# Layer 0's output projection in two parts, the first beside the threshold search, and layer 1's weight highs on another engine

## The reference

```python
h = rmsnorm(x, ev_norm)                       # then one input projection
ya = bg * causal_dwconv(cg * hv, conv_w)      # mixer A: features 0..511
yb = indexed_sparse_attention(...)            # mixer B: features 512..1023; top 256 keys by an indexer
x = x + concatenate([ya, yb]) @ w_out         # w_out: 1024 x 1024
x = x + conv_ffn(rmsnorm(x, ffn_norm), ...)   # D_FF = 2816
```

## Time and profile before

| what | us |
|---|---|
| median of 3 runs (2313.43 to 2315.07) | 2313.96 |
| the profiled execution's own time | 2312.72 |
| its span in the profile | 2310.9 |
| PE busy (share of the span) | 2127.4 (92%) |
| DVE busy | 1286.1 (56%) |
| POOL busy | 1098.9 (48%) |
| ACT busy | 940.6 (41%) |

### The profile page before, as it was taken

One profiled execution on the slowest core, in us unless ns is written; L12 is line 12 of the kernel. 1 busy time (PEld: TensorE's weight loads), 2 busy tenths in 40 slices (PEclk: granted clock), 3 DMA queues, 4 the chain that ended last, 5 costly groups with the idle time before them and its releaser, 6 DMA issues. The chain is left out here.

```text
span 2310.9 us, 29711 instructions
## 1 busy us (share of the span) xinstructions
PE 2127.4 (92%) x11534; PEld 1037.7 (45%) x11534; DVE 1286.1 (56%) x1955; ACT 940.6 (41%) x1385; POOL 1098.9 (48%) x729
## 2 busy tenths in 40 slices
PE   6989737899899999999989999679989999999998
PEld 3544325644344444444434444464434444444444
DVE  8788888735774156416634032884676416631652
ACT  5458956703562055215313212651355215521520
POOL 5113214124884667457585032013588456745642
PEclk8999969999999999999999999769999999999999
DMA  4002100011122112211232011002012111121112
GB/s 165 19 10 55 28 1 1 20 44 47 37 55 66 46 53 57 71 55 38 71 98 55 0 37 37 1 20 64 28 38 72 55 54 55 55 64 46 55 34 93
DMA packets 185986, 109.82 MB, mean 48 GB/s; under 512 B 3871, under 2 KB 180422, under 8 KB 185878
## 3 DMA queue, kind: packets, MB, share of 16 engines
q1 hardware_dynamic: 185414, 107.00, 15.9%
q0 software_dynamic: 464, 1.39, 0.2%
HBM read 104.18 MB, written 4.19 MB: 47 GB/s over the span
## 5 line engine op out<-in xcount | busy, mean ns | idle before, releaser
L626 POOL TENSOR_SCALAR w_scaled<-stage 128x1024 f32<-128x1024 f32 (+1 forms) x100 | 107.4, 1074 | 814.2 <-PE ps L890 504.5
L969 PE MATMUL ps<-h_hi,arena 128*128 128x512 f16 x1280 | 391.3, 381 | 11.6 <-DVE arena L2326 6.5
L890 PE MATMUL ps<-arena,w_hi 128*128 128x512 f16 x1504 | 388.0, 381 | 10.4 <-POOL w_lo L629 7.8
L969 PE MATMUL ps<-arena 128*128 128x512 f16 x1440 | 317.4, 379 | 0.1
L2282 DVE SCALAR_TENSOR_TENSOR xT<-ps,xT 128x1024 f32 (+1 forms) x64 | 78.3, 1224 | 409.3 <-PE ps L890 362.4
L969 PE MATMUL ps<-h_lo,arena 128*128 128x512 f16 x640 | 243.9, 381 | 0.0
L2335 DVE SCALAR_TENSOR_TENSOR work<-ps,fvec,work 128x1023 f32<-128x1023 f32 (+1 forms) x176 | 221.4, 1278 | 26.5 <-ACT work L1619 23.4
L890 PEld LDWEIGHTS ps<-arena,w_hi 128*128 128x128 f16 x1504 | 147.0, 98 | 191.0 <-POOL w_lo L629 11.2
L890 PE MATMUL ps<-arena,w_lo 128*128 128x512 f16 x752 | 224.6, 380 | 0.0
L969 PEld LDWEIGHTS ps<-arena 128*128 128x128 f16 x1440 | 140.8, 98 | 170.4 <-POOL arena L701 1.0
L969 PEld LDWEIGHTS ps<-h_hi,arena 128*128 128x128 f16 x1280 | 125.8, 98 | 166.5 <-issue 14.7
(11 more groups left out here) (363 smaller groups left out, 3819.9 us busy)
## 6 DMA issues: line engine op xcount, KB each, us to landing
stage<-in_ffn_w_up_dram SPq DMA_DIRECT2D x76, 512.0 KB, 4.2
stage<-in_ffn_w_down_dram SPq DMA_DIRECT2D x32, 512.0 KB, 4.2
stage<-in_od_w_in_dram SPq DMA_DIRECT2D x20, 512.0 KB, 3.7
stage<-in_ev_w_in_dram SPq DMA_DIRECT2D x12, 512.0 KB, 3.8
arena<-in_ffn_w_up_dram SPq DMA_DIRECT2D x12, 512.0 KB, 4.8
stage<-in_ffn_w_down_dram SPq DMA_DIRECT2D x16, 384.0 KB, 3.4
arena<-in_x_dram SPq DMA_DIRECT2D x8, 512.0 KB, 7.7
stage<-in_ev_w_out_dram SPq DMA_DIRECT2D x8, 512.0 KB, 3.9
```

The lines of the kernel that those rows point to most:

```text
L626: nc.gpsimd.tensor_scalar(scaled, src, W_SCALE, 1.0, ALU.mult, ALU.mult).then_inc(w_parts, 1)
L890: last = mm(out2[:, hf * HALF:(hf + 1) * HALF], w, a[:, k0 + k, hf * HALF:(hf + 1) * HALF], start=(first and k == 0 and pss == 0), stop=(l ...
L969: last = mm(ps[:, bank, :], left, right[:, k, :], start=(fresh and k == 0 and pss == 0), stop=(k == 3 and pss == 2), skip_group_check=True)
```

## The change

Layer 0's output projection runs in two parts. The first, `ev_out_a`, takes feature tiles 0 to 2 (of mixer A) of all eight units: it has eight unit numbers, eight ring uses and eight loads (192 KB) of its own, its splits stand on GpSimd between the mixer units' and the picks, and its matmuls on TensorE between the last mixer unit and the scores. VectorE adds each finished tile to `xT` in `add_early`: five in bits 26 to 30, one behind the search, one inside `resolve`, one behind it. `resolve` now stands ahead of `attend`. The scores wait for all eight adds. The second part takes feature tiles 3 to 7 where the whole was. Apart from that, the high parts of six of layer 1's eight token-major weight tiles (1 to 6) go from GpSimd to ScalarE, woven into its squares of the last down units.

```diff
-RESOLVE_AT = 1
+EARLY_KS = 3
+EARLY_BIT = 26
...
+        early_added, EARLY0 = rope_act, 7
...
-        order = [("ev_tm", 8, 0), ("ev_sc", 12, 12), ("ev_out", 8, 8), ...
+        order = [("ev_tm", 8, 0), ("ev_sc", 12, 12), ("ev_out_a", 8, 8), ("ev_out", 8, 8), ...
...
+        TM_HIGH_BY_ACT = (1, 2, 3, 4, 5, 6)
...
-            stream("ev_out", 2, 4, lambda i, u: (col_unit(t["ev_w_out"][0], i * 2 * P + u * P), 8))
+            stream("ev_out_a", 2, 4, lambda i, u: (col_unit(t["ev_w_out"][0], i * 2 * P + u * P)[:, 0:EARLY_KS], EARLY_KS))
+            stream("ev_out", 2, 4, lambda i, u: (col_unit(t["ev_w_out"][0], i * 2 * P + u * P)[:, EARLY_KS:], KT - EARLY_KS))
...
-                nc.gpsimd.tensor_scalar(hi, src, W_SCALE, 1.0, ALU.mult, ALU.mult).then_inc(w_parts, 1)
+                if not hi_by_act:
+                    nc.gpsimd.tensor_scalar(hi, src, W_SCALE, 1.0, ALU.mult, ALU.mult).then_inc(w_parts, 1)
                 pool.wait_ge(w_parts, n * 2 + 2)
...
-                        split(n, s, stage[:, s, :], w_scaled[:], otw_hi[:, i, :], otw_lo[:, i, :])
+                        split(n, s, stage[:, s, :], w_scaled[:], otw_hi[:, i, :], otw_lo[:, i, :], hi_by_act=i in TM_HIGH_BY_ACT)
...
             split_section("ev_sc", 6, 2, peeled=6)
+            split_section("ev_out_a", 2, 4, words=lambda u: EARLY_KS * P)
...
-            split_section("ev_out", 2, 4)
+            split_section("ev_out", 2, 4, words=lambda u: (KT - EARLY_KS) * P)
...
+            pe.wait_ge(a_mix, EARLY_KS)
+            for m in range(KT):
+                if m == 0:
+                    pe.wait_ge(a_f, 5)
+                elif m == 1:
+                    pe.wait_ge(a_cg, 5)
+                else:
+                    pe.wait_ge(early_added, EARLY0 + m - 1)
+                pe.wait_ge(w_split, unit0["ev_out_a"] + m + 1)
+                three_pass(m % 2, EARLY_KS, mix_hi, mix_lo, 0, pair(m % 2), True, True).then_inc(unit_done, 1)
+
             pe.wait_ge(a_f, 6)
+            pe.wait_ge(early_added, EARLY0 + KT)
...
-            out_projection("ev_out", 0, mix_hi, mix_lo, [(0, 8)], {})
+            out_projection("ev_out", 0, mix_hi, mix_lo, [(EARLY_KS, KT - EARLY_KS)], {})
...
-                residual_squares(24, 2)
+                for m in range(KT):
+                    if m + 1 in TM_HIGH_BY_ACT:
+                        n = woven("tm", m + 1)
+                        act.wait_ge(w_landed[n % 2], n * 8 + (16 - 8 * (n % 2)))
+                        act.wait_ge(w_split, n)
+                        A(otw_hi[:, m + 1, :], stage[:, n % 2, :], ACT.Copy, scale=W_SCALE).then_inc(w_parts, 1)
+                    act.wait_ge(x_added, m + 27)
+                    act.wait_ge(sq_added, m + 14)
+                    A(work[:, m % 2, :], xT[:, m, :], ACT.Square).then_inc(sq_ready, 1)
...
-            def resolve():
+            def resolve(between):
...
                 ts_(V.copy_predicated(back, srch_i[:, S_TAKE, allc], tr_))
+                between()
...
+            def add_early(m):
+
+                dve.wait_ge(unit_done, ring0["ev_out_a"] + m + 1)
+                V.scalar_tensor_tensor(out=xT[:, m, :], in0=pair(m % 2), scalar=W_UNSCALE, in1=xT[:, m, :],
+                                       op0=ALU.mult, op1=ALU.add).then_inc(early_added, 1)
+
             def mixer_part(bit):
+                if bit >= EARLY_BIT:
+                    add_early(bit - EARLY_BIT)
...
-                    if n == RESOLVE_AT:
-                        resolve()
...
             for bit in range(SEARCH_BITS):
                 search_bit(bit, lambda: mixer_part(bit))
+            add_early(KT - 3)
+            resolve(lambda: add_early(KT - 2))
+            add_early(KT - 1)
             attend()
+            dve.wait_ge(early_added, EARLY0 + KT)
```

More of the change, by code:

```diff
@@ L315, in build @@
         nu = nr = 0
-        order = [("ev_tm", 8, 0), ("ev_sc", 12, 12), ("ev_out", 8, 8), ("up0", 2, 2), ("plain0", 0, 2),
+        order = [("ev_tm", 8, 0), ("ev_sc", 12, 12), ("ev_out_a", 8, 8), ("ev_out", 8, 8), ("up0", 2, 2), ("plain0", 0, 2),
                  ("down0a", 8, 8), ("down0b", 8, 8), ("down0c", 0, 8), ("od_r_a", 0, 2),
@@ L616, in _, with split @@
             assert steps[0] == ROPE_STEPS, steps
-            def split(n, slot, src, scaled, hi, lo, ring=None):
+            def split(n, slot, src, scaled, hi, lo, ring=None, hi_by_act=False):
                 pool.wait_ge(w_landed[slot], n * 8 + (16 - 8 * slot))
```

## The result

The changed kernel takes 2290.48 us (median of 4 runs, 2289.36 to 2291.15) beside 2313.69 us of the kernel before on the same chip: 0.9899 of its time, 95% interval 0.9882 to 0.9916, or 23.2 us less. A second measurement on another chip gave 2291.40 beside 2313.88 us (0.9903, 0.9887 to 0.992). The forecast was 2288.0, with 2282 to 2298 as its range. Its form was right, part by part. What it lacked is a term for stretches whose code does not change.

What follows compares the result with a forecast made beforehand. TensorE was taken to bound the output projection, VectorE and ScalarE the search, GpSimd's period the woven stretch; -31.1 + 9.6 - 4.5 = -26.0 us from the 2313.96 us median gave 2288.0 us, range 2282 to 2298.

Steps and rivals of the forecast that it cites:

- Part 1: Output projection behind the attention: each of 8 units loses 18 of 48 matmuls, -31.1 us, bounds -31.1 and -28.
- supply rival: Output projection: load and split in series hold five-tile units at 10.35 us, no gain there, 2319.1 us; chance 0.04.
- rival that ends slower: The same weight-supply case in the output projection: the only one slower than before, deciding from a 9.7 us period; chance 0.04.
- Part 2: Early units in search and attention start: eight adds on VectorE and later head masks cost +9.6 us, bounds +8 and +13.
- head chain: Attention start: scores, mask to exp, exp to turn, turn put head 2's mask 1.9 us behind the last add.
- cold-units rival: Early units: pauses keep TensorE at 1.2 GHz throughout, VectorE waits for units, +8.6 us, 2296.6 us; chance 0.08.
- collision that the prediction had allowed for: Search with mixer: GpSimd's early splits collide with a VectorE tap pass or low part, 0 to 0.9 us, 0.3 taken.
- Part 3: Woven stretch: ScalarE makes six high parts, GpSimd's period falls from 8.97 to 8.0 us, -4.5 us, bounds -6 and 0.
- upper bound of -6: Woven stretch: GpSimd's low part stops colliding with VectorE's sum and TensorE sets 7.8 us per unit, -6 us.
- rival that the highs bring nothing: Woven stretch: square and high in one ScalarE queue delay the adds as much as GpSimd gains, 2292.5 us; chance 0.12.
- The sum: Whole kernel: -31.1 + 9.6 - 4.5 = -26.0 us, giving 2288.0 us.
- condition named in advance: Attention from head 2's mask to its end: a change in length of over 2 us would make the forecast wrong.

Runs made afterwards that it cites:

- e4: Changed kernel with one feature tile instead of three in the early part and seven behind the attention; 2309.32 us, 0.998 of before.
- e6: Changed kernel with the eight early evictions cut to one column each, all waits and matmuls kept; 2283.99 us.
- e3: Kernel before with only resolve moved ahead of the attention's first mask; 2316.09 us, 1.0005 of before.
- e5_again: Changed kernel unaltered, measured and profiled a second time; 2291.40 us.
- e2: Kernel before with only the high parts of layer 1's tiles 1 to 6 moved to ScalarE; 2307.76 us, 0.9975 of before.
- e1: Changed kernel with the high parts of tiles 1 to 6 given back to GpSimd; 2294.88 us, 0.9916 of before.
- e7: Changed kernel with 36 unread matmuls on TensorE between the last early unit and the first scores; 2290.22 us, 0.9896 of before.
- e11: e10 with the mixer's fourth feature tile also in early units 6 and 7; 2275.33 us, 0.9829 of before.
- e8: Changed kernel with 36 matmuls of the first two units behind the attention moved into TensorE's last attention pauses; 2286.31 us, 0.9881 of before.
- e10: e8 with unit 0 finished first, eviction 0 in bit 25, units 6 and 7 in other banks, resolve behind the second mask; 2282.17 us, 0.986 of before.

## Why the prediction was right, and where it was off

**Part 1** (-31.1 predicted, -31.34 measured). The working held: period 6.5 (6.48), TensorE the bound with no pause after its start, the half-clock start kept, the weight supply never late. e4 confirms the price of a tile to 0.05 us in 20.7. The supply rival is out. The rival that ends slower would have needed a period of 9.7 us.

**Part 2** (+9.6 predicted, +9.77 measured). The split was 8.1 for the evictions and 1.5 for the head chain (1.9 - 0.4). VectorE's timeline gives 8.0 and 1.7. The search is 4.6 us longer for its five evictions (4.65 in the prediction), from its end to the last eviction it is 2.3 us longer for the next two, and the last one holds VectorE for 1.1. Behind that one the first mask waits 0.56 us for its scores and the third comes 1.5 us behind the first, less the 0.41 us of masks moved. So it is the chain that was sized low; its four terms as written make 1.75 us and not 1.9, and about 2.1 was measured. e6 and e3 agree (7.35 with what the thin passes still take; 1.21 for the chain without the wait for scores). The steps in time came as written: search end near 314 (314.17), last addition near 329 (329.06), scores near 330 (330.44), no wait for a unit. The cold-units rival is out: the clock was 0.50 for the first two thirds of unit 1 (full from 288.4 us on) and 0.58 at the start of unit 6 (312 to 316 us), and full in the bursts between, and e4, with a third of the matmuls, has the same A to B.

GpSimd's timeline shows the collision that the prediction had allowed for; the second pair is the same two passes undisturbed:

```profile
264.62 1.17 POOL L631 TENSOR_SCALAR w_scaled<-stage 128x384 f32<-128x384 f32 x1 [6.01 <-PE ps L897]
265.76 1.47 POOL L633 TENSOR_SCALAR w_hi<-stage 128x384 f16<-128x384 f32 x1
...
274.98 0.51 POOL L631 TENSOR_SCALAR w_scaled<-stage 128x384 f32<-128x384 f32 x1 [6.75 <-PE ps L897]
275.45 0.51 POOL L633 TENSOR_SCALAR w_hi<-stage 128x384 f16<-128x384 f32 x1
```

Those two stood beside VectorE's taps, which read two arrays in SBUF (2.72 instead of 2.60 us). The loser was GpSimd; the path paid 0.12 us here and 0.11 at tile 3's taps (2.71 us), for 0.3 allowed. The Trainium skill (SBUF — State Buffer, section Who interferes with whom) says that a VectorE instruction with two SBUF inputs contends with a GpSimd instruction that reads SBUF. By that rule the trace agrees: the evictions, with one operand in PSUM, took 1.21 to 1.23 us throughout, and the GpSimd passes beside those at 291.28 and 298.67 us took their undisturbed 0.51 and 0.91 us.

**Part 3** (-4.5 predicted; -4.98, -4.92 and -5.12 measured in D to E, and -3.34 by the profile of e5_again). The size was nearly right for a partly wrong reason. The step that failed is "period 8.0, still over TensorE's 36 x 0.216 = 7.8 us", which left the low part at its disturbed 2.97 us. It came out at 2.13 us. VectorE's sum meets the scale pass of the down tile behind it instead, 1.59 us, where the earlier trace rows has 0.83. So the collision moved instead of going, and GpSimd's period of 7.73 us is a little under TensorE's 7.8: TensorE became the bound, as in the prediction's upper bound of -6, and its six units are 6.4 us shorter. What took 1.4 us of that back is the end of the stretch. The last addition starts 1.45 us behind TensorE's last matmul instead of at once, since the seventh sum stands ahead of it, and TensorE waits 1.6 us for that sum (L850 above); the prediction had 0.25. e2 has that wait too, and e1, without ScalarE's highs, has not. Two misses of opposite sign made the near hit. The norm's reciprocal comes 5.71 instead of 4.76 us behind E, but 21 us behind E that lag is gone, so E to F does not pay for it. The rival that the highs bring nothing is out.

**The sum** (-26.0 predicted, -23.2 measured; -22.5 on the second chip). The three edited columns give -26.55, so the miss between these two profiles lies in the unedited code, at which the sum had no term. B to C averages 145.4 us in the three kernels with the old order (before, e2, e3) and 146.0 in the six with the changed one and nothing more behind B (changed, e1, e4, e5, e6, e7). E to F averages 1088.9 and 1090.9. That is +0.6 and +2.0, and -26.5 + 2.6 = -23.9, close to what was measured. But in E to F the two groups overlap (1087.7 to 1089.4 and 1087.6 to 1093.0), and with e5_again in place of the first profile the edited columns alone give -24.8. The condition named in advance, attention longer by over 2 us, was not met (1.78). The kernel before happened to have the shortest attention of all thirteen profiles, which is luck on its side.

What makes E to F differ is not settled. VectorE's 524 instructions behind E are the same in all thirteen profiles. Set side by side they drift apart in layer 1's mixer, and from 545 us behind E on they keep their distance to within 0.4 us. What differs in the rows there is TensorE's granted clock. Busy time at the same place in the two profiles of the changed kernel, from 240 us behind E; first the changed kernel, then e5_again:

```profile
1430.00:1450.00 20.00, 15.69 (x188) 13.00 (x186) 17.17 (x34) 10.80 (x20) 0.00 (x0) 0.90 0.01 2
```

```profile
1433.00:1453.00 20.00, 18.80 (x202) 13.63 (x199) 14.06 (x26) 8.00 (x9) 0.00 (x0) 1.00 0.01 2
```

In the 60 us behind, the clock is at its 1.2 GHz level in both (0.50 and 0.51), and VectorE is busy for over 56 of them. Where it falls and rises shifts from one profile to the next. E to F goes by that and not by the edit alone: e2 (old order), e4 and e11 (changed order) have nearly the same clock through this stretch and 1087.6 to 1087.7 us. The Trainium skill (TensorE: Matmul & The Clock Gate, section What's actually happening) says that the turning point varies between runs of one kernel. By that, these columns would spread with no cause in the edit; the two profiles of one kernel differ by 1.0 us, the thirteen by 6.7. Whether the changed kernels' 2.0 us are chance or follow from when they reach the stretch would need many more profiles of each.

## What to carry to other kernels

Price a moved piece of work on the engine that sets the pace where it lands: 144 matmuls cost nothing beside the search, and the eight evictions behind them cost 8.0 us whatever they carried, so such a split pays by how much it moves per eviction. Then place each eviction in a wait that the pacing engine already has, and let the next stage wait only for those evictions whose banks it takes; the two together were worth 2.2 us here (e8 to e10). At the end of a stage, look for the part of the next one that does not need the last tile: filling 4.8 us of pauses with it gave 6.5 us, since the clock was kept too.

## What the runs showed of the hardware that was not expected

Warming TensorE ahead of a sparse stretch did not help: after 10 us at clock 1.00 the first heads of the attention still fell to 0.70 and 0.79, and the time was the same (e7). Keeping it warm into a dense stretch did: with the pauses filled up to the output projection the stretch 478 to 484 us ran at 1.00 instead of 0.55 (e8).

The collision between VectorE and GpSimd in the woven stretch was not removed by taking a pass from GpSimd. It moved to the pass that then stood beside VectorE's sum: from 2.97 us (2.13 undisturbed) in the low part to 1.59 (0.83 undisturbed) in the next scale pass.

A program's start moves too: mark A lay between 226.92 and 230.63 us in the thirteen profiles, over code that no kernel here edits. A difference of two whole spans has that in it, and one taken from mark to mark does not.
